# Moving the operands of four stages of a two-block transformer kernel to other byte remainders in SBUF

## What is computed

```python
# first block
h = x
h = h + nsa_mixer(rms(h, g0), ...)      # sparse attention: projections, compressed and windowed scores, o @ w_out
h = h + s5_mixer(rms(h, g1), ...)       # state space scan, gelu, y @ w_glu, gated, y @ w_out
h = rms(h, g_final)
# second block
h = h + even_mixer(rms(h, g2), ...)     # stick-breaking attention and retention, concat @ even_w_out
h = h + conv_ffn(rms(h, g3), ...)       # h @ w_up, causal conv of 3, silu, gate, @ ffn_w_down (2816 x 1024)
h = h + odd_mixer(rms(h, g4), ...)      # gated linear attention in chunks of 64, @ odd_w_out
h = h + conv_ffn(rms(h, g5), ...)
```

## The kernel before

| stage | activation (high, low) | where it is made |
|---|---|---|
| projections into a stage | `xh`, `xl` | norm or residual |
| attention output | `nh`, `nl` | `at` at L1043, L1044 |
| S5 gate product | `yh`, `yl` | `yh` at L2126, `yl` in a view at L2127 |
| S5 output | `gh`, `gl` | L2134, L2135 |
| even mixer output | `eo_h`, `eo_l` | L491, L492 |
| down projections (2) | `ghi`, `glo`, 22 chunks each | L402, L403 |
| odd mixer output | `ohi`, `olo` | L1733, L1734 |

## Time and profile before

### The profile page before, as it was taken

How to read it: one execution, slowest core, us unless ns; L and a number is a source line. 1 busy time by engine, 2 the same in 40 slices (tenths; PEclk the granted TensorE clock), 3 DMA queues, 4 the chain that set the end, 5 groups by cost and what they waited for, 6 DMA issues and landing times.

```text
span 1949.3 us, 26522 instructions
## 1 busy us (share of the span) xinstructions
PE 1925.5 (99%) x9866; PEld 1516.5 (78%) x9866; DVE 1145.5 (59%) x2077; ACT 578.3 (30%) x1118; POOL 796.1 (41%) x454
## 2 busy tenths in 40 slices
PE   8999999999999999999999999999999999999999
PEld 5967777788878776767688888886788888888887
DVE  5869998788874545666654444333645464444311
ACT  3226566416641134453221111101332231111000
POOL 3532222368854432222344444443233344444443
PEclk9999999999999999999999999999999999999999
DMA  5621101223122231111132222332112222222332
GB/s 182 186 76 34 44 34 34 76 92 104 42 69 96 88 124 55 56 64 65 65 102 97 97 97 97 108 98 97 65 65 76 72 92 97 97 97 97 108 119 76
DMA packets 54596, 167.66 MB, mean 86 GB/s; under 512 B 6864, under 2 KB 14928, under 8 KB 54112
## 3 DMA queue, kind: packets, MB, share of 16 engines
q1 hardware_dynamic: 46624, 155.21, 23.6%
q10 hardware_dynamic: 7872, 11.09, 2.1%
HBM read 157.90 MB, written 2.10 MB: 82 GB/s over the span
## 4 chain that ended last, share of the span: by engine, by line
PE 90%; DVE 8%; issue 1%; ACT 1%; DMA 1%; ACTq 0%; POOL 0%; DVEq 0%
PE bank L185 18%; PE bank L189 18%; PE bank L186 18%; PE bank L581 5%; PE bank L586 5%; PE bank L582 5%; DVE prob L1650 2%; DVE ssb L1637 2%; PE bank L1272 1%; PE bank L199 1%; PE bank L205 1%; PE bank L1297 1%; PE bank L202 1%; PE bank L2622 1%; PE bank L2611 1%
## 5 line engine op out<-in xcount | busy, mean ns | idle before, releaser
L168 POOL TENSOR_TENSOR wlo<-raw,whi 128x1024 fp32r<-128x1024 f32 x248 | 595.4, 2401 | 903.2 <-DVE whi L176 903.2
L176 DVE CAST whi<-raw 128x1024 fp32r<-128x1024 f32 x288 | 207.9, 722 | 339.4 <-PE bank L189 243.1
L185 PE MATMUL bank<-xh,whi 128*128 128x512 f32 x888 | 347.4, 391 | 0.0
L186 PE MATMUL bank<-xl,whi 128*128 128x512 f32 x888 | 345.8, 389 | 0.0
L189 PE MATMUL bank<-xh,wlo 128*128 128x512 f32 x888 | 220.3, 390 | 0.0
L185 PEld LDWEIGHTS bank<-xh,whi 128*128 128x128 f32 x888 | 166.8, 188 | 38.0 <-issue 3.6
L189 PEld LDWEIGHTS bank<-xh,wlo 128*128 128x128 f32 x888 | 167.6, 189 | 35.0
L186 PEld LDWEIGHTS bank<-xl,whi 128*128 128x128 f32 x888 | 166.9, 188 | 34.8 <-issue 0.5
L581 PE MATMUL bank<-xh,whi 128*128 128x512 f32 x424 | 175.3, 413 | 0.0
L582 PE MATMUL bank<-xl,whi 128*128 128x512 f32 x424 | 166.0, 392 | 0.0
L185 PE MATMUL bank<-ghi,whi 128*128 128x512 f32 x308 | 119.8, 389 | 0.0
(11 more groups left out here) (427 smaller groups left out, 3480.4 us busy)
## 6 DMA issues: line engine op xcount, KB each, us to landing
raw<-in_weights_dram SPq DMA_DIRECT2D x288, 512.0 KB, 3.2
h<-in_x_dram SPq DMA_DIRECT2D x2, 1024.0 KB, 7.1
out_dram<-h ACTq DMA_DIRECT2D x8, 256.0 KB, 2.0
etab<-in_even_tables_dram ACTq DMA_DIRECT2D x1, 1730.0 KB, 6.4
sz<-su SPq DMA_DIRECT2D x16, 64.0 KB, 2.0
sz<-su SPq DMA_DIRECT2D x16, 48.0 KB, 2.0
x_kh<-kvc_h ACTq DMA_DIRECT2D x2, 256.0 KB, 5.1
x_kl<-kvc_l ACTq DMA_DIRECT2D x2, 256.0 KB, 6.9
```

Of the source, the lines that this page charges most:

```text
L168: nc.gpsimd.tensor_tensor(wlo[:, s % 2, :], raw[:, s, :], whi[:, s % 2, :].bitcast(F32), ALU.subtract).then_inc(w_lo, 1)
L176: nc.vector.tensor_copy(whi[:, t_of_4 % 2, :], raw[:, t_of_4, :]).then_inc(w_hi, 1)
L185: nc.tensor.matmul(to, w_h[k], rhs_hi(k), start=first and k == 0, stop=False)
L186: nc.tensor.matmul(to, w_h[k], rhs_lo(k), start=False, stop=False)
```

## The change

It adds a number of bytes to the cursor of the shared region in four stages, so all that the stage places behind that point lies so many bytes higher. No instruction is added, removed or moved; only addresses change, and lines behind L1043 have a number higher by one.

```diff
@@ the feed-forward's tensors
-        used[0] = base
+        used[0] = base + 32
         ghi = at("ghi", [P, FT, S], F32R)
@@ the even mixer's tensors
-        used[0] = base
+        used[0] = base + 96
         eo_h = at("eo_h", [P, KC, S], F32R)
@@ the attention's tensors
         nin = at("nin", [P, 5, S])
+        used[0] += 224
         nh = at("nh", [P, KC, S], F32R)
@@ the odd mixer's tensors
-        used[0] = base
+        used[0] = base + 160
         ohi = at("ohi", [P, KC, S], F32R)
```

## The result

| | before | changed kernel |
|---|---|---|
| median of the runs | 1950.51 us (4 runs) | 1960.08 us (1959.57 to 1961.62, 4 runs) |
| ratio | | 1.0049, 95% interval 1.0037 to 1.0061 |
| span of the profiled execution | 1949.3 us | 1957.8 us |
| TensorE busy | 1925.5 us | 1934.9 us |
| VectorE, ScalarE, GpSimd busy | 1145.5, 578.3, 796.1 us | 1144.3, 578.2, 796.7 us |

A forecast was written before the change was run, and what follows sets the result against it. TensorE was taken to bound the kernel. Moved large matmuls gave +5.9 us and all other terms 0, so 1956.3 us against the 1950.43 median; the range went from 1945 to 1966.

The forecast's parts named there:

- What bounds the kernel: Whole kernel: TensorE busy 1925.5 of 1949.3 us, so added nanoseconds on each large matmul arrive at the end nearly whole.
- The reading that the distance of the addresses decides: Large matmuls: activation-to-weights address distance sets the step, 226.7 ns at 0, 228.9 at 64, 231.7 mixed.
- rival B: All moved stages: nothing changes, 1950.4 us, as two S5 stages could be slower for another reason; chance 0.22.
- Term 1: 1632 matmuls with moved activations, in down and output projections: 3.6 ns more each, +5.9 us.
- Term 2: Small products of the mixers and attention, whose operands move: 0, with 4.5 us kept as bound.
- Term 3: Projections between small products (L581, L1213): addresses kept, settling after moved small products unchanged, 0.
- Terms 4 and 5: VectorE and ScalarE reading moved starts: at most 1.5 us, 0 taken; DMAs into moved tiles: 0.
- Rival C: Moved stages faster: half a step of shift frees 6.7 ns a matmul, -10.9 us, 1939.5; chance 0.12.
- Rival D: Moved stages much slower: starts 32 bytes off the 64-byte grid lengthen each matmul's read, +19.6 us, 1970.0; chance 0.14.
- The signs in the profile: Tile distance in moved stages rises from 5.44 to 5.49 to 5.56 us; `xh` stays 5.44, S5 5.493 and 5.56.
- Each with a pattern of its own: Down and output projections: each moved stage's tile distances would rise with a different pattern.
- case A: Moved stages lose the 226.7 ns step: +3.6 to +8.2 us, 1954.0 to 1958.6; the forecast itself, chance 0.52.

The follow-up runs named there:

- the attention run: Kernel before with only the attention's tensors behind `nh` and `nl` moved by 224 bytes; output projection began at 360.25 us against 360.07, no kernel time given.
- the S5 run: Kernel before with `yl` read 192 bytes further and `gh`, `gl` 64 bytes lower, all at distance 0; 1948.00 us against 1950.96, ratio 0.9984.

## Why the prediction was right, and where it was off

- *What bounds the kernel* held. Nanoseconds on the large matmuls came out at the end whole: the stages with moved tiles take 10.15 us longer in the trace (twice 3.52, and 1.05, 0.97 and 1.10), and the span 8.5, which is that less the earlier start of 1.8 and small differences.
- *The reading that the distance of the addresses decides*, which the prediction called an inference from three stages, is now shown from three sides: the weights moved alone make `xh` slow and leave `ghi` fast, S5 brought to distance 0 becomes 5.44, and `ghi` at 64 has exactly the step of `gh`. The same runs settle rival B: the step of a matmul depends on where its two operands lie to each other, by 2.2 to 10 ns in 227. What inside TensorE or SBUF makes it so stays an inference. The Trainium skill (SBUF — State Buffer, section "Who interferes with whom") says that TensorE never waits on another engine and that its read ports for the streaming operand and for the weights are independent. The runs do not bear out the second half as far as time goes: the weights moved alone cost 29.9 us.
- *Term 1 was mis-sized.* The forecast took 3.6 ns for each of 1632 matmuls, the middle between the steps at 64 and of the mixed S5 stage; the moved stages measured 6.7 ns (5.60 us a tile), and 7.6 at distance 160. The step that failed was the middle itself. The forecast read 64 and the mixed stage as lower and upper bound for a distance of 32, since "a half step of 32 seems to me no better placed than the whole one of 64": it is three times as costly, and 64 is the cheapest place besides 0. With 6.7 ns the term would have been 1632 x 6.7 = 10.9 us. The mixed stage was no bound for it: its two distances, 0 and 64, are the two best, and most of its 5.0 ns is a price of mixing, since 64 alone costs 2.2. Mixing can also lie below the worse of the two: 0 with 32 gives 5.52 us a tile where 32 alone gives 5.60. The 48 matmuls of each output projection that begin between small products cost almost nothing more: the six dense tiles give 6 x 0.16 = 0.96 us of the 1.05 and 0.97 measured, and at distance 160 they give all of the 1.10. Down projections 7.1 measured against 1056 x 6.7 = 7.1.
- *Term 2, small products:* 0 forecast; 0 by the attention run, within 0.2 us; 0.10 us in the even mixer and at most 0.03 in the odd one, with the projections between them.
- *Term 3, settling of the projections between small products:* 0 forecast. It lies in the same stretches, so it is no more than that. The settling itself is real: behind the 316 ns of the earlier trace rows the starts follow by 231, 231, 236, 228, 232, 231 ns and then by 226 or 227.
- *Terms 4 and 5:* VectorE's and ScalarE's busy times differ by 1.2 and 0.1 us, and the waits for DMAs are the same six, none longer by more than 0.6 us. 0 as forecast.
- *Rival C* fell with the table: no distance gives a step under 226.7 ns. *Rival D* (12 ns each) did not come either: with the weights at the same remainder, `ghi` off the 64-byte grid keeps its 5.44 us, and the worst distance, 4 bytes, costs 10 ns. `sx`, given as evidence against it, said little: its products have 128 columns, and the small products whose operands moved did not react.
- The signs in the profile were the right ones to name. The moved tiles rose to 5.60 and 5.62, past the 5.56 that A allowed, `xh` stayed at 5.44 and S5 at 5.493 and 5.56. "Each with a pattern of its own" did not come: three of the four distances give the same 5.60.

The time, 1960.1, lies past the 1954.0 to 1958.6 of case A. It lies within the range because that adds 4.5 us for the small products and reaches into D, and neither of these came; and a part of the 10.15 us was hidden by the earlier start of the attention. The kind of the effect was foreseen; its size was taken as 3.6 ns where it was 6.7, and that the range held the time is in part luck.

## What to carry to other kernels

Where fp32r matmuls of 512 columns run back to back with a weight load of 128 x 128 behind each, put both operands at the same remainder of 256 bytes; here that is worth 1 to 4% of each such matmul, for one line in an allocator. Check it in the trace by the distance from tile to tile, which is exact to a few nanoseconds in one look, while the time of the whole kernel needs many runs to tell 0.2%. If an operand's place can't be chosen, a view into a longer row or a tile moved down into free bytes may do it, as in S5.

## What the runs showed of the hardware that was not expected

- The cost of the distance is not monotonic and not a matter of one grid: 4 bytes cost 10.0 ns a matmul, 16 bytes 5.0, 64 bytes 2.2, 128 bytes some 6, 160 bytes 7.6. Where the tiles repeat exactly, their step is a whole multiple of 13.33 ns, which is 16 ticks of 1.2 GHz: to the nanosecond the starts in the traces give 5440, 5493, 5520, 5547, 5560, 5600 and 5680 ns, 408 to 426 of them. Within a tile the starts repeat as well, at distance 64 with nearly 226, 229 and 232 ns over three matmuls. At 128, 160 and 208 the tiles themselves differ by up to 15 ns. What in the two reads has this grain was not tested.
- The profile's durations of the weight loads don't show it. In the changed kernel those of `ghi` are 187 and 188 ns as before; only the matmuls' starts move apart, and with them the modelled ends (395 ns for 389).
- Three stretches in which the granted clock changes differ from trace to trace by up to 1 or 1.5 us, more than some of the effects studied: when the clock rises in the gate products at the start (5.18 to 6.61 us for eight matmuls), when and how long it falls at the attention's first small products (0.76 or 0.88 of full speed from 128 to 142 us), and how long at the odd mixer's start (1.5 us more in the S5 run and in the one at multiples of 64, 1.3 in the one at odd multiples of 16). In each of the three, runs whose addresses in that stage are the same differ, so the addresses are not needed for it.

Left open: why a distance of 0 is the best one, whether it stays so with the weights at remainders other than the two tried (128 and 96), and whether other types, such as bf16, or matmuls of another number of columns with both operands moved apart react in the same way.
